# Gathered expert rows transposed by ScalarE copies and VectorE 32x32 transposes instead of TensorE, with the expert loop written in pairs of blocks

## What is computed

```python
def run_block(args):
    toks, e = args
    xb = h_pad[toks]                                              # 128 gathered rows of 1024
    return (jax.nn.silu(xb @ w_gate[e]) * (xb @ w_up[e])) @ w_down[e]   # 1024 -> 256 -> 1024

ys = lax.map(run_block, (slot_tok.reshape(n_blocks, MOE_BLOCK), block_e))
ys = ys.reshape(n_slots, -1) * slot_w[:, None]
out = jnp.zeros((T + 1, ys.shape[1])).at[slot_tok].add(ys)[:T]
```

## Time and profile before

| | us |
|---|---|
| median of 3 timed runs | 2897.6 |
| lowest and highest | 2897.42, 2899.65 |
| span of the profiled execution | 2897.5 |
| TensorE busy (matmul) | 2851.8 |
| VectorE busy | 1575.9 |
| ScalarE busy | 816.7 |
| GpSimd busy | 871.3 |

### The profile page before, as it was taken

How to read it: one execution, slowest core, us unless ns; L and a number is a source line. 1 busy time by engine, 2 the same in 40 slices (tenths; PEclk the granted TensorE clock), 3 DMA queues, 4 the chain that set the end, 5 groups by cost and what they waited for, 6 DMA issues and landing times.

```text
span 2897.5 us, 38361 instructions
## 1 busy us (share of the span) xinstructions
PE 2851.8 (98%) x12809; PEld 1883.5 (65%) x12809; DVE 1575.9 (54%) x4155; ACT 816.7 (28%) x1550; POOL 871.3 (30%) x1366
## 2 busy tenths in 40 slices
PE   8999999999999999999999999979999999999997
PEld 6776777777767767776777677744444444444443
DVE  5656565556555565556565656563444444444444
ACT  2223232322332232323232323222222222222222
POOL 1021111112111211121112111114656665665665
PEclk9999999999999999999999999989999999999999
DMA  7312121211122111211121211267675667567653
GB/s 308 141 52 72 60 74 52 73 70 63 52 73 76 56 59 66 81 52 59 66 81 52 73 59 66 75 224 266 235 267 186 227 202 253 200 222 274 237 171 124
DMA packets 109623, 369.01 MB, mean 127 GB/s; under 512 B 39497, under 2 KB 41426, under 8 KB 99442
## 3 DMA queue, kind: packets, MB, share of 16 engines
q1 hardware_dynamic: 48946, 252.91, 23.9%
q0 software_dynamic: 60480, 113.57, 11.9%
HBM read 325.09 MB, written 140.33 MB: 161 GB/s over the span
## 4 chain that ended last, share of the span: by engine, by line
PE 97%; DMA 1%; DVE 0%; issue 0%; ACT 0%; SPq 0%; POOL 0%; POOLq 0%; DVEq 0%; ACTq 0%
PE PB L368 24%; PE PB L1591 19%; PE PB L379 16%; PE PB L463 12%; PE SS L1631 9%; PE YB L463 4%; PE TB L1576 2%; PE YB L417 2%; PE TB L357 1%; DMA arena<-in_w_in 1%; PE SS L426 1%; PE TB L440 1%; PE SS L430 1%; PE TB L404 1%; PE YB L1624 1%; PE MB L408 1%
## 5 line engine op out<-in xcount | busy, mean ns | idle before, releaser
L368 PE MATMUL PB<-arena,hT 128*128 128x512 f32 (+2 forms) x2112 | 726.8, 497 | 1.7 <-DVE arena L1118 0.9
L368 PEld LDWEIGHTS PB<-arena,hT 128*128 128x128 f32 x2112 | 397.9, 191 | 270.5 <-issue 222.7
L1591 PE MATMUL PB<-arena,hT 128*128 x1296 | 569.3, 592 | 0.0
L379 PE MATMUL PB<-hT,arena 128*128 128x128 f32 x4224 | 487.2, 276 | 4.4 <-DVE arena L1106 4.4
L379 PEld LDWEIGHTS PB<-hT,arena 128*128 128x128 f32 x4224 | 481.8, 193 | 8.2 <-issue 4.6
L1591 PEld LDWEIGHTS PB<-arena,hT 128*128 128x128 f32 x1296 | 246.1, 190 | 309.8 <-issue 309.8
L1143 POOL TENSOR_SCALAR rs<-sq 128x2 f32<-128x2 f32 (+1 forms) x66 | 14.2, 215 | 1304.2 <-ACT h L735 958.0
L463 PE MATMUL PB<-arena,tT 128*128 128x274 f32 (+1 forms) x1056 | 357.8, 493 | 0.7 <-ACT tT L639 0.7
L1631 PE MATMUL SS<-arena,xdt 128*128 x640 | 287.9, 592 | 0.0
L463 PEld LDWEIGHTS PB<-arena,tT 128*128 128x128 f32 x1056 | 195.5, 190 | 140.8 <-issue 120.5
L808 DVE SCALAR_TENSOR_TENSOR xc<-xT,cols,xc 128x128 f32<-128x128 f32 x792 | 216.8, 347 | 3.5
(11 more groups left out here) (273 smaller groups left out, 3585.7 us busy)
## 6 DMA issues: line engine op xcount, KB each, us to landing
arena<-in_w_expert SPq DMA_DIRECT2D x32, 2048.0 KB
arena<-in_w_expert SPq DMA_DIRECT2D x32, 1024.0 KB
h_rows<-h SPq DMA_DIRECT2D x34, 512.0 KB, 2.7
x_in<-in_x_rows SPq DMA_DIRECT2D x33, 512.0 KB, 4.6
hT<-in_x_cols SPq DMA_DIRECT2D x33, 512.0 KB, 3.7
x_res<-in_x_rows SPq DMA_DIRECT2D x33, 512.0 KB, 5.1
dec<-running_sums SPq DMA_DIRECT2D x33, 512.0 KB, 3.7
first_rows<-bc SPq DMA_DIRECT2D x33, 512.0 KB, 3.9
```

Of the source, the lines that this page charges most:

```text
L368: mm = nc.tensor.matmul(out, hT[u][:, k, :], w_group(name)[:, k, :], start=k == 0, stop=k == KD - 1)
L379: mm = nc.tensor.matmul(PB[b][:, c * P:(c + 1) * P], w_block(name, c)[:, k, :], hT[u][:, k, :], start=k == 0, stop=k == KD - 1)
L1591: mm = nc.tensor.matmul(PB[u][:, :], hT[u][:, k, :], arena[:, bass.ds(slot + k * 2 * DE, 2 * DE)], start=k == 0, stop=k == KD - 1)
```

## The change

Block rows from block 2 on are no longer transposed by TensorE. A 128x128 transpose is split in 32x32 squares, which a VectorE instruction transposes each for itself; a square whose quarter (group of 32 partitions) changes must also be moved. ScalarE copies three of the four quarters of the gathered rows (`move`, twelve copies of 32 partitions by 256 elements per block, into `zz` and `btok`), and one VectorE transpose of 512 and one of 256 elements on all 128 partitions turn them into `hT` (`turn_moved`). The fourth quarter is transposed by four VectorE instructions of 32 partitions by 256 elements that read `g_buf` and write each of the four quarters of `hT` (`turn_last`). The loop body is now one pair of blocks on every engine, and takes nothing from the pair after it on TensorE; the down projection of odd blocks goes to the PSUM banks (`TB`) that the row transposes no longer need. The order of the DMAs and roots on GpSimd is also new, and the last norm of both blocks of a pair is now done in the next pair. Left out below: renamed and reused semaphores, the constants of the last pair, and the row transposes of blocks 0 and 1, which stay.

```diff
         def pe_phase2(pe):
-            def step(b):
-                u = b % 2
-                pe_gate_up(pe, b + 1)
...
-                for k in range(2):
-                    mm = nc.tensor.transpose(YBv[:, k, :], hb2[u][:, k * P:(k + 1) * P], ident)
-                mm.then_inc(s["hbT_full"], 1)
-                pe_rows(pe, b + 2)
-                pe.wait_ge(s["hbT_out"], b + 1)
...
+            def pair(j):
+                b = 2 * j
+                weights = weights0 if j == 0 else pe_weights(pe, b)
+                if j > 0:
+                    pe_gate_up(pe, b, weights, 0, KD)
+                later = pe_weights(pe, b + 1)
+                pe_gate_up(pe, b + 1, later, 0, 4)
+                pe_hidden(pe, b)
+                pe_gate_up(pe, b + 1, later, 4, KD)
+                pe_down(pe, b, weights[0], 0, 3)
+                pe_hidden(pe, b + 1)
+                pe_down(pe, b, weights[0], 3, 4)
+                pe_down(pe, b + 1, later[0], 0, 4)
...
         def act_phase2(act):
+            def move(b, n0, n1):
+                if n0 == 0:
+                    act.wait_ge(gathered[b % GB], 16 * (b // GB + 1))
+                    after(act, s["rows_turned"], b - 2)
+                for n in range(n0, n1):
+                    g, q = n // 4, n % 4
+                    ins = nc.scalar.activation(moved[g][32 * q:32 * (q + 1), :], quarter(b, g, q), ACT.Copy)
+                if n1 == 12:
+                    ins.then_inc(s["rows_moved"], 1)
...
+            def pair(j):
+                b = 2 * j
+                silu(b)
+                if j > 0:
+                    squares(0, b - 1)
+                move(b + 2, 0, 12)
+                hidden(b)
+                if j > 0:
+                    squares(1, b, b - 1)
+                silu(b + 1)
+                move(b + 3, 0, 7)
+                hidden(b + 1)
+                weigh(b)
+                move(b + 3, 7, 12)
+                weigh(b + 1)
...
         def dve_phase2(dve, st):
+            def turn_last(b):
+                dve.wait_ge(gathered[b % GB], 16 * (b // GB + 1))
+                dve.wait_ge(s["gu_full"], b)
+                for q in range(4):
+                    V.transpose(hT[b % 2][32 * q:32 * (q + 1), :, 96:128],
+                                quarter(b, 3, q))
+
+            def turn_moved(b):
+                dve.wait_ge(s["rows_moved"], b - 1)
+                V.transpose(hT[b % 2][:, :, 0:64].rearrange("p c (g t) -> p g c t", g=2),
+                            zz[:, :].rearrange("p (g c i) -> p g c i", g=2, i=32))
+                V.transpose(hT[b % 2][:, :, 64:96], btok[:, :].rearrange("p (c i) -> p c i", i=32)).then_inc(s["rows_turned"], 1)
...
+            def pair(j):
+                b = 2 * j
+                if j > 0:
+                    add_first(0, b - 1, 16 * j)
+                gate(b)
+                if j > 0:
+                    add_first(1, b, 16 * j)
+                turn_last(b + 2)
+                if j > 0:
+                    norm(0, b - 1)
+                turn_moved(b + 2)
+                gate(b + 1)
+                turn_last(b + 3)
+                if j > 0:
+                    norm(1, b)
+                weigh(b)
+                add_x2(b)
+                turn_moved(b + 3)
+                weigh(b + 1)
+                add_x2(b + 1)
...
         def pool_phase2(pool):
-            def step(b):
-                gather(b + AHEAD)
-                if b > 0:
-                    pool.wait_ge(s["fin_sq"], b)
-                    root_of(1 - b % 2, b)
-                for k in range(2):
-                    pool.wait_ge(s[f"dn_out{k}"], b + 1)
-                rows_to(first_d[:, :], y_buf[b % GB], first_i, b, first_kept)
-                residual(b + 1)
-                if b > 0:
-                    pool.wait_ge(s["fin_out"], b)
-                    store(b - 1)
-                earlier(b + 1)
+            def keep(b):
+                for k in range(2):
+                    pool.wait_ge(s[f"dn_out{k}"], b + 1)
+                rows_to(first_d[:, :], y_buf[b % GB], first_i, b, first_kept)
...
+            def finish(b):
+                pool.wait_ge(s["fin_sq"], b + 1)
+                root_of(b % 2, b + 1)
+                pool.wait_ge(s["fin_out"], b + 1)
+                rows_to(y_out, f_buf[b % 2], last_i, b, y_stored[b % 2])
+
+            def pair(j):
+                b = 2 * j
+                gather(b + 4)
+                gather(b + 5)
+                earlier(b)
+                if j > 0:
+                    finish(b - 2)
+                    finish(b - 1)
+                keep(b)
+                residual(b + 2)
+                earlier(b + 1)
+                keep(b + 1)
+                residual(b + 3)
```

More of the change, by code:

```diff
@@ L1379, in over_pairs @@
                     branches.enter_context(eng.If(j < used))
[L1380 to L1381 removed]
+                    pair(j)
             return used
@@ L1551, in pool_phase2 @@
             residual(0)
[L1552 to L1559 removed]
+            residual(1)
+            used = over_pairs(pool, pair)
+            last_n = pair_ends(pool, used)
+            for u in range(2):
+                pool.wait_ge(s["fin_sq"], last_n[u])
+                nc.gpsimd.tensor_tensor(spare[:, 1:2], neg_half[:, 0:1], neg_half[:, 0:1], ALU.mult)
+                root_of(u, last_n[u])
+                pool.wait_ge(s["fin_out"], last_n[u])
+                nc.gpsimd.tensor_tensor(spare[:, 2:3], neg_half[:, 0:1], neg_half[:, 0:1], ALU.mult)
+                rows_to(y_out, f_buf[u], final_i, u, y_stored[u])
             half_up = pool.value_load(misc[0:1, 3:4], min_val=(SURE + 1) // 2, max_val=(PAIRS + 1) // 2)
@@ L1656, in silu, with hidden, squares, weigh @@
                 nc.scalar.activation(silu_g[u], PB[u][:, 0:DE], ACT.Silu).then_inc(s["silu_out"], 1)
-            def step(b):
+            def hidden(b):
                 act.wait_ge(s["hbT_full"], b + 1)
-                after(act, s["dn_full"], b + 1)
-                nc.scalar.activation(hTb, YBv, ACT.Copy).then_inc(s["hbT_out"], 1)
-                silu(b + 1)
-                rows0(b + 2)
-                if b > 0:
-                    squares(b - 1, b)
+                after(act, s["dn_full"], b if b > 1 else 0)
+                nc.scalar.activation(hTb[b % 2], YBv, ACT.Copy).then_inc(s["hbT_out"], 1)
+            def squares(u, added, before=None):
+                if u:
+                    act.wait_ge(s["fin_sq"], before)
+                act.wait_ge(s["first_added"], added)
+                nc.scalar.activation(h2[:, :], f_buf[u], ACT.Square, accum_out=sq[:, u:u + 1]).then_inc(s["fin_sq"], 1)
+            def weigh(b):
                 act.wait_ge(s["dn_full"], b + 2)
@@ L1676, in act_phase2 @@
-            used = over_pairs(act, step)
-            squares(1, 2 * used)
+            used = over_pairs(act, pair)
+            last_n = pair_ends(act, used)
+            for u in range(2):
+                squares(u, last_n[u], last_n[0])
         def dve_phase2(dve, st):
             def rows1(b):
-                u = b % 2
                 dve.wait_ge(s["gx_T"], 2 * b + 2)
-                after(dve, s["gu_full"], b)
-                V.tensor_copy(hT[u][:, half(1), :], TB[1][:, :, :]).then_inc(s["gx_out1"], 1)
+                V.tensor_copy(hT[b][:, half(1), :], TB[1][:, :, :]).then_inc(s["gx_out1"], 1)
@@ L1725, in dve_phase2 @@
             rows1(1)
-            gate(0)
             dve.wait_ge(gf_loaded, 16)
-            used = over_pairs(dve, step)
-            dve.wait_ge(s["x2_added"], 2 * used)
-            V.memset(spare[:, 3:4], 0.0)
-            add_first(1, 16 * used)
-            norm(1, 2 * used)
+            used = over_pairs(dve, pair)
+            last_n = pair_ends(dve, used)
+            for u in range(2):
+                V.memset(spare[:, 3 * u:3 * u + 1], 0.0)
+                add_first(u, last_n[u], 16 * used)
+            for u in range(2):
+                norm(u, last_n[u])
         def sp_end(sp):
```

139 lines of the change are left out of this document (68 added, 71 removed).

## The result

| | before | after |
|---|---|---|
| median of the timed runs, us | 2898.6 (4 runs) | 2935.0 (4 runs) |
| lowest and highest, us | 2897.42, 2900.59 | 2923.84, 2942.49 |
| span of the profiled execution, us | 2897.5 | 2934.4 |
| mean granted TensorE clock in it | 0.992 | 0.985 |

The changed kernel takes 1.0122 times as long (95% interval 1.0100 to 1.0145), some 36 us more. The prediction was 2930.

A forecast was written before the change was run, and what follows sets the result against it. GpSimd's ordered loop, waiting for keeps to land and for norms, was taken to bound the changed kernel, not TensorE: 1962.5 + 19.2 + 21.0 + 904.4 (38 x 23.8) + 23.3 = 2930 us, range 2840 to 2995.

The forecast's parts named there:

- to keep(0): From the loop's first product to the first keep on GpSimd: 17.6 us plus weighing and late start, 19.2 us.
- first turn: From keep(0), pair 0 having nothing to finish, pair 1 follows at TensorE's pace of 21.0 us.
- 38 turns: GpSimd's loop from one even block's keep to the next: 23.8 us each, above TensorE's 21.0; 904.4 us together.
- keep(78) to the last store: Last pair on GpSimd after the loop, its keep, roots, norms and stores: last store starts 18.3 us after keep(78).
- from there to the end of the span: From the last store's start to the end of execution: 5.0 us, taken from the profile before.
- meetings: GpSimd's indirect DMAs wait for VectorE's two-input additions, 2.04 in place of 1.02 us: 0.5 us a turn, 1.5 at longest.
- longest turn: Upper bound of GpSimd's turn, with landings of 7 us both times and 1.5 for meetings: 25.3 us.
- rival 4: VectorE's transposes cost two cycles an element: 1.9 us more between norms, turn 25.7, time 3002 us; chance 0.12.
- the two waits that the prediction named: In GpSimd's loop: for a keep to land, 5.9 us after its start, and for VectorE's norm, no longer hidden.
- the 16 us that the prediction held ready for it: If VectorE's transposes also blocked GpSimd, the turn would be about 0.4 us longer and the sum 16 us higher.
- ScalarE, by order: Seven moves and the next hidden copy queue behind the wait for turn_moved(b + 2); if late, TensorE is late; unpriced.
- "TensorE keeps up" rival: GpSimd's chain stays below TensorE's 21.0 us a pair, so the time falls to 2820 us; chance 0.10.

The follow-up runs named there:

- runs 1: Changed kernel without the last norm's root on GpSimd; VectorE's norm multiplies by a constant and waits for the squares directly: 2902.1 us, 1.0014 of the kernel before.
- run 2: Changed kernel with the keeps scattered to another HBM array, so the gather of first_d needs no landing wait: 2897.5 us, 1.0001 of the kernel before.
- run 3: Changed kernel with only the order of GpSimd's instructions in a pair changed, so other work lies over its waits: 2912.2 us, 1.0045 of the kernel before.
- run 10: Changed kernel with only the y store reading a constant tile, so VectorE's add_x2 waits for no store: 2954.2 us, 1.0206 of the kernel before.
- run 6: Kernel before, block by block, with row transposes moved to ScalarE and VectorE and hidden transposes between two gate-up halves: 2831.9 us, 0.9775 of the kernel before.

## Why the prediction was right, and where its steps were not

Sign and size were right, 2930 against a median of 2935.0. By its own sum (profiled execution, us):

| step | predicted | measured |
|---|---|---|
| first product of the loop | 1962.5 | 1960.9 |
| to keep(0) | 19.2 | 19.4 |
| first turn | 21.0 | 27.8 |
| 38 turns | 904.4 | 897.5 |
| keep(78) to the last store | 18.3 | 16.8 |
| from there to the end of the span | 5.0 | 11.9 |
| sum | 2930 | 2934.4 |

So part of the agreement is chance: +14 us that the sum did not have, -10 us of terms that were too large. Two figures beside the sum were off in themselves. With 7 us for both landings and 1.5 for meetings its own steps give a longest turn of 26.7, not 25.3, and 5.8 us to either side of the kernel before are turns of 22.8 to 23.1, not 22.85 to 23.15.

*What was right.* 640 row transposes and the gate-up of block 80 left TensorE. The transposes were priced one element a cycle, 0.42, 0.69 and 0.42 us, and measured 0.44, 0.71 and 0.40: rival 4 is out. From 256 to 512 elements it is 0.31 us more, where 0.27 was priced and 0.54 would be two cycles. So the trace, to within this difference, now agrees with the page "Vector Engine (DVE) Microarchitecture Reference" of the Trainium skill (section 3.8), one element per cycle per lane. GpSimd's loop is what made the kernel slower, by the two waits that the prediction named: runs 1 and 2 take one each, and the excess goes. The meetings on GpSimd are real too, and only those with two-input additions cost: of 387 indirect DMAs between 1990 and 2900 us 47 took over 1.5 us (up to 2.10, against 1.01), and all 47 began while a `TENSOR_TENSOR` of two SBUF tiles ran on VectorE; of the 107 that began during a transpose none took over 1.08. So transposes don't block GpSimd, and the 16 us that the prediction held ready for it stay at nothing.

*The turn.* 23.8 was predicted and 23.6 measured (38 turns). Term by term: keep to `earlier(b+1)` 5.9 against a mean of 5.0; `earlier` to keep 1.3 against 1.6; keep to `earlier(b+2)` 6.2 against 5.9; from there to the first store 4.1 against 4.2; store to store 4.5 against 5.1; store to keep 1.3 against 1.8. The first was taken from the kernel before, where other work sits between; here the wait for a keep ended as early as 3.0 us after its start (2324.02 to 2327.04), where 4.9 was the lower bound.

*The failed picture behind it.* The prediction saw the same GpSimd chain of 23.8 in every turn. In 27 of 39 the chain hardly shows: they take 22.8, and TensorE waits 1.19 us for ScalarE's copy and only 0.08 for the gate, which is where GpSimd's lateness would reach it (on VectorE the gate stands behind the norm); the mean is made by 12 turns of 25.9. In all 39 TensorE is idle for 1.8 us a turn, not 2.8, and busy for 21.9, not 21.0.

Two terms are missing there. The first is the clock, which no term had (the text named it as what would make it wrong): 17 us by the windows. The second is a step that the sum put at nothing, "ScalarE, by order": seven moves before the second hidden copy, of which the prediction said that TensorE is late if the wait before them is. They are late without it. In the turn shown `turn_moved(b + 2)` is done at 2316.43, the moves start at 2317.12, the hidden transposes end at 2318.97 and the copy starts at 2320.08. The moves were priced at 0.38 us and run at 0.42 from start to start (2.95 us for seven), which is 0.3 of the 0.78 us that TensorE stands; the rest is their place. TensorE waits for this copy in 38 pairs, 48.4 us in all between 2000 and 2880 us. Therefore the "TensorE keeps up" rival had the wrong floor, 21.0: with one of GpSimd's waits gone the turn is 22.6, and the 38 x 1.6 = 61 us from there to 21.0 did not come back in run 2. The page "ScalarE: Activation LUTs" of the Trainium skill (section "What ACT_TABLE_LOAD costs") gives, measured on 128 partitions, 186 ns and 0.833 ns an element for an ACTIVATE with immediate scale and bias, of which about 93 ns overlap with the next. An estimate from it is 0.31 us from start to start for 256 elements, by which the copy of the turn shown would have been just in time. The moves here, of 32 partitions, measured 0.42, and the measurement decides.

*A wait not named.* `add_x2` on VectorE waits until the store that read its buffer two blocks ago has landed; in the changed kernel store and keep stand next to each other, and VectorE stands for 81.6 us between 2000 and 2880 us (27.5 in the kernel before), with the residual gather behind it:

```profile
DVE arena L1793 <- DMA out_y<-arena,bc: 81.6, 37, 6.5
...
POOL xT L1508 <- DVE arena L1793: 32.0, 10, 6.0
```

Run 10 shows that taking it away alone gains nothing.

*The first turn.* "Pair 0 has nothing to finish, so pair 1 follows at 21.0" was wrong by 6.8 us: keep(0) needed over 10 us to land.

```profile
1980.30 1.35 POOL L1513 DMA_INDIRECT first_rows<-x_res,bc  x1 [16.24 <-ACT x_res L1723]
1981.95 1.01 POOL L1508 DMA_INDIRECT xT<-x_rows,bc  x1 [0.31 <-issue]
1991.11 0.99 POOL L1508 DMA_INDIRECT xT<-first_rows,bc  x1 [8.15 <-DMA first_rows<-x_res,bc]
```

Between 1980 and 1990 us the DMA engines are busy for 0.99 of the time (368 GB/s). A median landing from the middle of the loop doesn't hold where the weights of the first experts are still coming in.

*The end.* 5.0 us from the last store to the end was taken from the earlier trace rows; 11.9 were measured, the 7 us told of under run 3, which stay open.

## What to carry to other kernels

Before work is taken off the engine that bounds, ask which dependent copy that work was covering: here 70 us of removed transposes were worth 3 us alone, not clear of noise, and 66 us once something else stood in the gap. An engine that issues transfers in order needs its waits spread out: with the stores and the keep of two blocks in one chain GpSimd was idle for 205 us before its 80 stores, and in run 6, block by block, for 25. And cost an engine loop with a spread, since a few long turns hurt twice, once by the wait and once by the clock after it.

## What the hardware showed

- The clock: 1.3 us after the end of a wait of 3.56 us the granted clock fell to 0.50 for 6.8 us, and eight records of products took 6.12 us in place of 3.6. In the loop of the changed kernel this adds up to 34 us at 1.2 GHz, in six stretches behind waits of 1.7 to 4.1 us; the kernel before, without waits, has none there.
- An indirect DMA that GpSimd issues while VectorE adds two SBUF tiles can take up to 2.10 us in place of 1.01 (47 of 387 took over 1.5, all in such a meeting); one issued during a 32x32 transpose took 1.08 at most (107 cases).
- Copies of 32 partitions on ScalarE, source and target in SBUF, take 413 ns for 256 elements and follow each other every 0.42 us, while 128 partitions by 256 elements from PSUM take 384 ns (line 1711).
- The gather that waits for a scatter of 512 KB to land started 3.9 us after the scatter's start in the turn shown (2301.44 to 2305.33), and 10.8 us after it when the DMA engines were busy for 0.99 of the time (1980.30 to 1991.11).
